# Norms by token halves, the first queries for 128 tokens first, and other homes for the gathered rows

## The chip, the core and the metric

The kernel runs on one core of one Trainium2 chip. The metric is its device time in microseconds (us). The core's engines are TensorE (PE; its weight loads are listed as PEld), VectorE (DVE), ScalarE (ACT), GpSimd (POOL) and SyncE (SP, which here only issues DMAs). A matrix product in full fp32 shows as two passes of PE; one in fp32r, on operands split into a high and a low part, as three products of one pass each.

## The reference

256 tokens of 1024 channels run through two layers (feed-forward, mixer, feed-forward), then one block of another kind, whose second half is an expert layer:

```python
for i in range(2):
    x = x + 0.5 * rmsnorm(swiglu_ffn(rmsnorm(x, pre1[i]), ...), post1[i])
    x = x + rmsnorm(mixer(rmsnorm(x, mix_pre[i])), mix_post[i])
    x = x + 0.5 * rmsnorm(swiglu_ffn(rmsnorm(x, pre2[i]), ...), post2[i])
h = rms_norm(x, norm1); merged = gated sum of mLSTM branch and RG-LRU branch
x = x + merged @ w_out
h2 = rms_norm(x, norm2)
q = h2 @ w_q                                # 8 heads, 2 x 128 each
scores = q . sub_keys                       # 128 keys for each half
idx, gate = best 16 of 16 x 16 sums         # per token and head
x = x + sum_k gate_k * gelu(u[idx_k] . h2) * v[idx_k]
out = rms_norm(x, final_norm)
```

With 8 heads of 16 experts each token needs 128 rows of `u` and 128 rows of `v`, each of 1024 fp32 numbers.

## The kernel before

Weights come in blocks of 1 MB (1024 x 256), each into one of `SLOTS` = 6 ring buffers `m.raw`; SP loads a block when the one six places earlier is used. `RING.first` gives a stage's first block. The residual lies by token, `m.x_tok[:, h, :]` with h the half of 128 tokens, and each half has two 512-channel parts d. All engines run programs written out in order (`tensor_program`, `scalar_program`, `vector_program`, `pool_program`, `sync_program`), joined by semaphores (`S.name.by` sets, `wait_ge(*S.name.at(...))` waits), so an instruction is late for all that is queued behind it on its engine.

**Seams.** At the end of a feed-forward or mixer the product is in PSUM banks 4 to 7, half 0 complete some us before half 1. `vector_post_norm` and `scalar_post_norm` (L646 to L681) take squares (ACT, L656), gain (DVE, L675), root (ACT, L659) and the residual add (DVE, L681), half after half. Then the residual is turned to channel-major by PE (`tensor_turn`, L752 to L767): for `mix` and `norm1` with a diagonal of the inverse norms (so the squares, `scalar_token_squares` L695, one root for both halves L706 and `vector_diagonals` L714 come first), for `pre1` and `pre2` plainly, where the norm follows as a row of factors after the first product block (`tensor_factor_row`, L721). `tensor_keep_going` (L743) lets PE multiply ones meanwhile: `before` products ahead of half 0's turn and `between` products ahead of half 1's. ACT makes the high part of the turned operand (`scalar_high`, L789), DVE the low part (`vector_low`, L797); the first product block (`tensor_split_block`, L451 to L453) waits for the low part of each pair of tiles. In layer stages `mix` the low parts of the weights are made by POOL (`pool_mix_rest`, L407), two blocks ahead and before the seam; in the FFNs by DVE (L443).

**The start.** SP issues x, two weight blocks and 22 small parameter loads. DVE makes mask constants (`vector_constants`, L531 to L545), PE turns the parameters when the last has landed (`tensor_params`, L613), runs 8 products of ones, and turns x.

**Output projection and queries.** `tensor_w_out` (L2273) multiplies half 0 by all four blocks of `w_out`, then half 1; DVE adds each half to the residual (L2329). Then the `norm2` seam for both halves, and `tensor_scores`: for each of 8 heads one block of `peer_w_q` times 256 tokens (L360), the turned `h` for the experts in quarters (L2375), and the scores (L2388), which ACT copies out (L2396). The weights of the queries come through the ring, each when a `w_out` or query block six places earlier is used.

**Experts.** `HEAD_TURNS` takes the 8 heads of half 0, then of half 1. `vector_choose` (L2470 to L2488, on DVE) makes one turn's 16 indices. `pool_experts` issues, for 32 groups of 8, the gathers of `u` rows of group i and then the `v` rows of group i-1 (L2539; one gather fetches one row for each of 128 tokens, 512 KB). DVE dots each `u` row with h (L2548); `v` rows are weighed and summed, four of each group by PE (L2641) and four by DVE (L2585). Row r goes to home r modulo the number of homes, and waits until the row before it there is done. There are 12 homes for `u` and 17 for `v` (`PeerMemory`): 16 in `m.proj`, 12 in ring slots that are free when a query block is used, one in `m.operand`. At group 0 DVE takes the first choice, then the second between its dots.

## Time and profile before

| | us |
|---|---|
| median of 3 runs (2656.16 to 2657.62) | 2656.24 |
| the profiled execution, its own time | 2657.05 |
| its span, first to last instruction | 2655.8 |

```profile
PE 2269.2 (85%) x13786; PEld 1932.1 (73%) x13786; DVE 1759.4 (66%) x3266; ACT 970.9 (37%) x1550; POOL 807.2 (30%) x671
...
PE   6999999999999999999999999999898544444445
...
DVE  5555894665556556894665555243429998989986
```

The first line gives busy time, share of the span and instruction count for each engine. The others cut the span into 40 slices of 66.4 us; a digit is the busy share of a slice in tenths. Waits are shown in brackets behind a timeline row: how long the engine had been idle and what released it. The granted clock of PE is given as a share of 2.4 GHz.

### The profile page before, as it was taken

The numbers are of one execution on the slowest core, as the hardware profiler recorded it, in microseconds if no ns is written. First come the engines' busy times: TensorE is split into PE (matmuls) and PEld (weight loads), VectorE is DVE, ScalarE is ACT, GpSimd is POOL, SyncE is SP. The second block draws the span as 40 slices with busy tenths as digits, with TensorE's granted clock in tenths as the row PEclk, the third lists the DMA queues.
The fourth block names the chain that finished last, engine by engine and source line by source line (L and its number), as shares of the span: only waits on it lengthen the run. The fifth ranks groups of instructions, "written<-read, shape, count | busy, mean of one in ns | idle before, by whom it ended". The sixth has DMA issues, their size and how long they took to land.

```text
span 2655.8 us, 34386 instructions
## 1 busy us (share of the span) xinstructions
PE 2269.2 (85%) x13786; PEld 1932.1 (73%) x13786; DVE 1759.4 (66%) x3266; ACT 970.9 (37%) x1550; POOL 807.2 (30%) x671
## 2 busy tenths in 40 slices
PE   6999999999999999999999999999898544444445
PEld 6998998998998998998998998888766211111111
DVE  5555894665556556894665555243429998989986
ACT  4345554454335435553454432342213111111111
POOL 1005772000000005771000000000007777777774
PEclk9999999999999999999999999999999677777767
DMA  6567994025554567993024554443249999999997
GB/s 212 183 179 129 188 167 131 33 74 177 183 183 160 188 171 129 187 174 117 33 94 155 184 190 144 141 139 106 74 150 399 419 419 419 419 418 418 419 419 314
DMA packets 316369, 560.29 MB, mean 211 GB/s; under 512 B 16296, under 2 KB 233394, under 8 KB 316210
## 3 DMA queue, kind: packets, MB, share of 16 engines
q1 hardware_dynamic: 242482, 289.63, 39.7%
q0 software_dynamic: 73728, 268.47, 24.9%
q8 instruction: 109, 1.79, 0.3%
q14 instruction: 50, 0.41, 0.1%
HBM read 557.00 MB, written 1.05 MB: 210 GB/s over the span
## 4 chain that ended last, share of the span: by engine, by line
PE 65%; DVE 13%; POOL 8%; DMA 7%; issue 3%; ACT 3%; SPq 0%; DVEq 0%; ACTq 0%; POOLq 0%
PE banks_to L853 11%; PE bank L451 7%; PE bank L452 7%; PE bank L453 7%; PE bank L360 6%; POOL proj L2539 5%; PE banks_and L360 4%; DMA proj<-in_peer_v,gdn_conv 4%; DMA weights<-in_peer_v,gdn_conv 3%; POOL weights L2539 3%; DVE banks_to L1054 3%; PE banks_and L451 3%; PE banks_and L452 3%; PE banks_and L453 3%; PE banks_to L1246 2%
## 5 line engine op out<-in xcount | busy, mean ns | idle before, releaser
L407 POOL TENSOR_TENSOR weights_low<-weights,weights_high 128x1024 fp32r<-128x1024 f32 x128 | 306.1, 2423 | 683.3 <-ACT weights_high L370 682.8
L453 PE MATMUL bank<-operand_hi,weights_low 128*128 128x256 f32 x1792 | 508.5, 284 | 0.0
L451 PE MATMUL bank<-operand_hi,weights_high 128*128 128x256 f32 x1776 | 505.2, 284 | 3.6 <-DVE operand_lo L797 3.3
L452 PE MATMUL bank<-operand_lo,weights_high 128*128 128x256 f32 x1776 | 503.6, 284 | 0.0
L370 ACT CAST weights_high<-weights 128x1024 fp32r<-128x1024 f32 x392 | 386.6, 1046 | 7.0 <-DMA weights<-in_ffn_w_in 6.7
L443 DVE TENSOR_TENSOR weights_low<-weights,weights_high 128x1024 fp32r<-128x1024 f32 x264 | 308.2, 1221 | 91.3 <-ACT weights_high L370 91.3
L451 PEld LDWEIGHTS bank<-operand_hi,weights_high 128*128 128x128 f32 x1776 | 339.1, 191 | 7.0 <-issue 4.7
L453 PEld LDWEIGHTS bank<-operand_hi,weights_low 128*128 128x128 f32 x1792 | 342.9, 191 | 0.0
L452 PEld LDWEIGHTS bank<-operand_lo,weights_high 128*128 128x128 f32 x1776 | 337.5, 190 | 1.3
L453 PE MATMUL banks_and<-operand_hi,weights_low 128*128 128x256 f32 x768 | 217.6, 283 | 0.0
L451 PE MATMUL banks_and<-operand_hi,weights_high 128*128 128x256 f32 x752 | 213.7, 284 | 3.6 <-DVE operand_lo L797 3.3
L452 PE MATMUL banks_and<-operand_lo,weights_high 128*128 128x256 f32 x752 | 212.7, 283 | 0.0
L2548 DVE CUSTOM_DVE_ANT_0 proj<-proj,banks_to 128x1024 f32<-128x1024 f32 x172 | 207.7, 1212 | 5.1 <-DMA proj<-in_peer_u,gdn_conv 4.9
L2539 POOL DMA_INDIRECT proj<-in_peer_u,gdn_conv x172 | 162.8, 947 | 90.0 <-issue 43.6
L2613 ACT ACTIVATE gdn_conv<-gdn_conv 128x8 f32<-128x8 f32 x32 | 6.7, 210 | 486.6 <-DVE gdn_conv L2548 486.6
L1054 DVE SCALAR_TENSOR_TENSOR banks_to<-proj,cnv_dw_cols,banks_to 128x254 f32<-128x254 f32 (+28 forms) x464 | 181.0, 472 | 0.0
L360 PE MATMUL bank<-operand,weights 128*128 128x256 f32 x736 | 161.8, 379 | 0.0
L2074 POOL TENSOR_TENSOR proj<-proj 128x512 f32<-128x512 f32 x4 | 5.6, 1420 | 493.9 <-ACT proj L2297 493.9
L360 PEld LDWEIGHTS bank<-operand,weights 128*128 128x128 f32 x736 | 139.4, 190 | 18.7
L451 PEld LDWEIGHTS banks_and<-operand_hi,weights_high 128*128 128x128 f32 x752 | 143.0, 190 | 5.1 <-issue 3.9
L453 PEld LDWEIGHTS banks_and<-operand_hi,weights_low 128*128 128x128 f32 x768 | 146.6, 191 | 0.0
L452 PEld LDWEIGHTS banks_and<-operand_lo,weights_high 128*128 128x128 f32 x752 | 142.5, 189 | 0.4
(524 smaller groups left out, 4402.6 us busy)
## 6 DMA issues: line engine op xcount, KB each, us to landing
weights<-in_ffn_w_in SPq DMA_DIRECT2D x88, 1024.0 KB, 5.1
weights<-in_mix_w_in SPq DMA_DIRECT2D x64, 1024.0 KB, 12.5
weights<-in_ffn_w_out SPq DMA_DIRECT2D x44, 1024.0 KB, 5.0
...
```

The costliest lines, as they stand in the source:

```text
L360: ins = t.matmul(out, raw[:, k, q * P:(q + 1) * P], x[:, k, :], start=(k == 0), stop=(k == KT - 1))
L370: S.high.by(X.scalar.copy(halves(high)[q], halves(m.raw[b % SLOTS])[q]), b, q)
L407: S.rest.by(X.gpsimd.tensor_tensor(halves(m.low[b % SLOTS])[q], halves(m.raw[b % SLOTS])[q], halves(mix_high(m, l, i))[q].bitcast(F32), AL ...
L443: S.low.by(X.vector.tensor_tensor(halves(m.low[b % SLOTS])[q], halves(m.raw[b % SLOTS])[q], halves(ffn_high(m, stage, i))[q].bitcast(F32), ...
L451: t.matmul(out, w_hi, x_hi, start=start, stop=False, skip_group_check=skip)
L452: t.matmul(out, w_hi, x_lo, start=False, stop=False, skip_group_check=skip)
L453: return t.matmul(out, w_lo, x_hi, start=False, stop=stop, skip_group_check=skip)
L853: ins = X.tensor.matmul(y_part(m, h, d), x(k)[:, at], w[:, k, d * 512:d * 512 + 512], start=start and k == 0 and n == 0, stop=last and k = ...
L1054: ins = v.scalar_tensor_tensor(out=acc(c)[:, s:NT], in0=glu(c)[:, 0:NT - s], scalar=weight(k, c), in1=acc(c)[:, s:NT], op0=ALU.mult, op1=A ...
L1246: ins = X.tensor.matmul(out[:, j, :], lhsT(j), rhs(j), start=True, stop=True)
L2539: landed[r % len(homes)].by(X.gpsimd.indirect_dma_start(out=home, out_offset=None, in_=table, in_offset=at), r)
L2548: S.dotted.by(X.vector.tensor_tensor_reduce(out=u, in0=u, in1=K.h_tok[:, n // HEADS, :], scale=1.0, scalar=0.0, op0=ALU.mult, op1=ALU.add, ...
```

## The change

It has these parts:

- **Token norms by halves.** Each half gets its own mean (on DVE), root (on ACT, with that mean as bias), reciprocal and diagonal. For `pre1` and `pre2` the roots and diagonals come ahead of the FFN's loop, no longer within it.
- **Order of the residual adds.** Half 1's gain goes between half 0's two adds.
- **Turn.** For `mix` and `norm1` no products of ones between the halves, 20 instead of 12 ahead, and tile pairs 0 and 1 of both halves before pairs 2 and 3. For `pre1` and `pre2` 10 ahead and 5 between instead of 8 and 8.
- **Entry block.** The first product block waits for each tile's high part, takes both products with it for both column halves, and takes the product with the low part of x last, over all tiles.
- **POOL** makes one mixer block's low part ahead of the seam, and the others after the last residual add of `post1`.
- **Start.** The second weight block is loaded behind the parameters; PE turns x and runs 12 products of ones before it turns the parameters; ACT squares x first; DVE makes its constants after the split of block 1. The parameters' columns go to banks 6, 7, 0, 1.
- **Output projection.** Half 0, then two of half 1's eight units, half 0's norm and turn and its first query (`tensor_half_turn`, `tensor_query_half`, `tensor_half_scores`, each for 128 tokens) between further units, then the rest. Three heads are done by halves. DVE takes choice 0 before it adds half 1 (`vector_output(X, m, S, 1)`).
- **Query weights 2 to 6** are loaded into `m.proj` when the last mLSTM output is made, ahead of `w_out`'s blocks 2 and 3; query 7 into the slot of `w_out`'s first block.
- **Homes.** `u` has 6 homes in `m.proj` and 4 in the slots of `w_out` blocks 1 and 2; `v` has 19, in the slots of `w_out` 3 and queries 0 and 1, the homes of query weights 2 to 6, the slot of `w_out` 0 with query 7's weights, and `m.operand`.

```diff
-GROUP, U_ROWS, V_ROWS = 8, 12, 17
+GROUP, U_ROWS, V_ROWS = 8, 10, 19
 DVE_ALONE, EARLY = 0, 2
...
+QUERY_HOMES = {2: 48, 3: 56, 4: 24, 5: 0, 6: 8}
+LAST_QUERY = 7
...
-        first = RING.first["peer_q", 2]
-        late = [(flat(m.raw[(first + j) % SLOTS][:, 4 * i:4 * i + 4, :]), first + j) for j in range(2, HEADS) for i in range(2)]
-        self.u = [(rows[:, s, :], None) for s in range(G)] + late[0:4]
-        self.v = [(rows[:, G + s, :], None) for s in range(G)] + late[4:12]
-        self.v += [(flat(m.operand[:, 0:4, :]), first + HEADS - 1)]
+        first, out = RING.first["peer_q", 2], RING.first["w_out", 2]
+        slot = lambda b: [(flat(m.raw[b % SLOTS][:, 4 * i:4 * i + 4, :]), b) for i in range(2)]
+        query = lambda n: [(rows[:, QUERY_HOMES[n] // 4 + i, :], first + n) for i in range(2)]
+        self.u = [(rows[:, s, :], None) for s in (4, 5, 8, 9, 10, 11)] + slot(out + 1) + slot(out + 2)
+        self.v = slot(out + 3) + slot(first) + slot(first + 1) + query(2) + query(3) + query(4) + query(5) + query(6)
+        self.v += [(home, first + LAST_QUERY) for home, _ in slot(out)] + [(flat(m.operand[:, 0:4, :]), first + LAST_QUERY)]
...
+def tensor_entry_block(X, m, S, b, high, low, n):
+
+    bank, x = b % BANKS, m.split_x
+    X.bank_free(bank)
+    out = lambda q: m.bank[bank][:, q * NT:(q + 1) * NT]
+    for q in range(2):
+        X.pe.wait_ge(*low.at(b, q))
+    for k in range(KT):
+        X.pe.wait_ge(*S.x_high.at(n, k))
+        for q in range(2):
+            hi, lo = halves(high)[q], halves(m.low[b % SLOTS])[q]
+            X.tensor.matmul(out(q), hi[:, k, :], x.hi[:, k, :], start=k == 0 and q == 0, stop=False, skip_group_check=True)
+            X.tensor.matmul(out(q), lo[:, k, :], x.hi[:, k, :], start=False, stop=False, skip_group_check=True)
+    for k in range(KT):
+        if k % 2 == 0:
+            X.pe.wait_ge(*S.x_low.at(n, k // 2))
+        for q in range(2):
+            ins = X.tensor.matmul(out(q), halves(high)[q][:, k, :], x.lo[:, k, :], start=False, stop=k == KT - 1, skip_group_check=True)
+    S.used.by(ins, b)
...
+def vector_gain_branch(X, m, S, n, ready, c, h):
+
+    v, w, gain, other = X.vector, X.dve, m.gain_row[GAIN_ROWS[n[0]]], m.sums[:, 2 * h + 1:2 * h + 2]
+    w.wait_ge(*ready[h])
+    for d in range(2):
+        _, at = part(h, d)
+        if d:
+            w.wait_ge(*S.squares_act.at(n, h, 1))
+            S.mean.by(v.tensor_scalar(other, other, mean_of(c), c * RMS_EPS, ALU.mult, ALU.add), n, h)
+        S.gained.by(v.tensor_tensor(m.spare_tok[:, h, at], y_part(m, h, d), gain[:, at], ALU.mult), n, h, d)
...
+    vector_gain_branch(X, m, S, n, ready, c, 0)
+    vector_add_branch(X, m, S, n, 0, 0)
+    vector_gain_branch(X, m, S, n, ready, c, 1)
+    vector_add_branch(X, m, S, n, 0, 1)
+    vector_add_branch(X, m, S, n, 1, 0)
+    vector_add_branch(X, m, S, n, 1, 1)
...
+def scalar_token_norm(X, m, S, n, ready, scratch):
+
+    scalar_token_squares(X, m, S, n, 0, ready, scratch)
+    scalar_token_squares(X, m, S, n, 1, ready, scratch)
+    scalar_token_root(X, m, S, n, 0)
+    scalar_token_root(X, m, S, n, 1)
...
-def tensor_boundary(X, m, S, n, first, ready, scaled, before, between):
+def tensor_boundary(X, m, S, n, first, ready, scaled, before):
 
     tensor_keep_going(X, m, before, first % BANKS)
-    tensor_turn(X, m, S, n, 0, first, ready, scaled)
-    tensor_keep_going(X, m, between, first % BANKS)
-    tensor_turn(X, m, S, n, 1, first, ready, scaled)
+    if scaled:
+        for pairs in ((0, 1), (2, 3)):
+            for h in range(2):
+                tensor_turn(X, m, S, n, first, ready, scaled, h, pairs)
+    else:
+        tensor_turn(X, m, S, n, first, ready, scaled, 0, range(4))
+        tensor_keep_going(X, m, before // 2, first % BANKS)
+        tensor_turn(X, m, S, n, first, ready, scaled, 1, range(4))
...
-            ins = X.scalar.activation(m.split_x.hi[:, k, :], m.bank[b][:, q * NT:(q + 1) * NT], ACT.Copy, scale=gain[:, k:k + 1])
-        S.x_high.by(ins, n, i)
+            S.x_high.by(X.scalar.activation(m.split_x.hi[:, k, :], m.bank[b][:, q * NT:(q + 1) * NT], ACT.Copy, scale=gain[:, k:k + 1]), n, k)
...
-            if j == 0:
-                scalar_token_root(X, m, S, pre_norm_of(stage))
...
-    sync_rows(X, m, S, first["w_out", 2], io["w_out_2"], 0)
+    sync_rows(X, m, S, first["w_out", 2], io["w_out_2"], 0, (0, 1))
+    X.sp.wait_ge(*S.mlstm_dve.at("y", 3))
+    for i, n in enumerate(QUERY_HOMES):
+        S.query_in[i].by(X.sync.dma_start(query_weights(m, n), columns(io["peer_w_q_2"], 0, n * 256)), n)
+    sync_rows(X, m, S, first["w_out", 2], io["w_out_2"], 0, (2, 3))
...
-    for i in range(HEADS):
+    for i in (0, 1):
         sync_load(X, m, S, first + i, columns(io["peer_w_q_2"], 0, i * 256))
+    X.sp.wait_ge(*S.used.at(RING.first["w_out", 2]))
+    S.query_in[-1].by(X.sync.dma_start(query_weights(m, LAST_QUERY), columns(io["peer_w_q_2"], 0, LAST_QUERY * 256)), LAST_QUERY)
     X.sp.wait_ge(*S.used.at(first + HEADS - 1))
...
+def tensor_output_and_scores(X, m, S, K):
+
+    units = [(i, k) for i in range(4) for k in range(2)]
+    tensor_w_out(X, m, S, 0, units)
+    tensor_w_out(X, m, S, 1, units[0:2])
+    tensor_half_turn(X, m, S, 0)
+    tensor_w_out(X, m, S, 1, units[2:3])
+    tensor_query_half(X, m, S, 0, 0)
+    tensor_w_out(X, m, S, 1, units[3:4])
+    tensor_half_scores(X, m, S, K, 0, 0)
+    tensor_w_out(X, m, S, 1, units[4:8])
+    for n in (0, 1):
+        tensor_turn_quarter(X, m, S, "h", m.operand, n, 4 + n)
+    tensor_query_half(X, m, S, 1, 0)
+    tensor_query_half(X, m, S, 2, 0)
+    tensor_half_scores(X, m, S, K, 1, 0)
+    tensor_half_turn(X, m, S, 1)
+    tensor_half_scores(X, m, S, K, 2, 0)
+    tensor_query_half(X, m, S, 0, 1)
+    tensor_query_half(X, m, S, 1, 1)
+    tensor_half_scores(X, m, S, K, 0, 1)
+    tensor_query_half(X, m, S, 2, 1)
+    tensor_half_scores(X, m, S, K, 1, 1)
+    for n in (2, 3):
+        tensor_turn_quarter(X, m, S, "h", m.operand, n, 4 + n)
+    tensor_query(X, m, S, HALVED)
+    tensor_half_scores(X, m, S, K, 2, 1)
+    for n in range(HALVED + 1, HEADS):
+        tensor_query(X, m, S, n)
+        tensor_head_scores(X, m, S, K, n - 1)
...
+def scalar_output_and_scores(X, m, S, K):
+    scratch, ready = m.early_sum[:, :].rearrange("p (t d) -> p t d", t=1).to_broadcast([P, 2, KT * P]), block_added_at(S)
+    scalar_token_squares(X, m, S, "norm2", 0, ready, scratch)
+    scalar_token_root(X, m, S, "norm2", 0)
+    scalar_half_operand(X, m, S, 0)
+    scalar_query_half(X, m, S, K, 0, 0)
+    scalar_half_scores(X, m, S, K, 0, 0)
+    scalar_query_half(X, m, S, K, 1, 0)
+    scalar_token_squares(X, m, S, "norm2", 1, ready, scratch)
+    scalar_token_root(X, m, S, "norm2", 1)
+    scalar_query_half(X, m, S, K, 2, 0)
+    scalar_half_scores(X, m, S, K, 1, 0)
+    scalar_half_operand(X, m, S, 1)
+    scalar_half_scores(X, m, S, K, 2, 0)
+    scalar_choose(X, m, S, K, 0)
+    scalar_query_half(X, m, S, K, 0, 1)
+    scalar_query_half(X, m, S, K, 1, 1)
+    scalar_half_scores(X, m, S, K, 0, 1)
+    scalar_query_half(X, m, S, K, 2, 1)
+    scalar_half_scores(X, m, S, K, 1, 1)
+    scalar_gelu(X, m, S, K, 0)
+    scalar_choose(X, m, S, K, 1)
+    scalar_query(X, m, S, K, HALVED)
+    scalar_half_scores(X, m, S, K, 2, 1)
+    scalar_gelu(X, m, S, K, 1)
+    for n in range(HALVED + 1, HEADS):
+        scalar_query(X, m, S, K, n)
+        scalar_head_scores(X, m, S, K, n - 1)
...
+def vector_output(X, m, S, h):
+    vector_add_output(X, m, S, h)
+    vector_token_mean(X, m, S, "norm2", h)
+    vector_diagonal(X, m, S, "norm2", h)
+    vector_half_operand(X, m, S, h)
...
-    X.dve.wait_ge(*S.score_pe.at("h", 3))
+    vector_output(X, m, S, 1)
+    X.dve.wait_ge(*S.score_pe.at("h", 1))
     choice = vector_choose(X, m, S, K, 1)
     for i in range(GROUPS):
         if i % 2 and i // 2 + 2 < CHOICES:
             choice = vector_choose(X, m, S, K, i // 2 + 2)
+        if i == HALF:
+            X.dve.wait_ge(*S.score_pe.at("h", 3))
...
-    sync_ffn(X, m, S, ("ffn1", 0), 0, io["ffn1_w_in"], io["ffn1_w_out"], range(AHEAD))
+    sync_ffn(X, m, S, ("ffn1", 0), 0, io["ffn1_w_in"], io["ffn1_w_out"], range(1))
     sync_layer_params(X, m, S, io, 0)
+    sync_ffn(X, m, S, ("ffn1", 0), 0, io["ffn1_w_in"], io["ffn1_w_out"], range(1, AHEAD))
...
-    tensor_params(X, m, S, 0)
     for l in range(LAYERS):
-        tensor_to_split(X, m, S, ("pre1", l), ("ffn1", l), x_ready_at(S, l), False, 8, 8 if l else 0)
-        tensor_ffn(X, m, S, ("ffn1", l), split_at(S, ("pre1", l)))
+        tensor_to_split(X, m, S, ("pre1", l), ("ffn1", l), x_ready_at(S, l), False, 10 if l else 0)
+        if not l:
+            tensor_keep_going(X, m, 12, 1)
+            tensor_params(X, m, S, 0)
+        tensor_ffn(X, m, S, ("ffn1", l))
         y_taken(X, S, ("post1", l))
-        tensor_to_split(X, m, S, ("mix", l), ("glu", l), added_at(S, ("post1", l)), True, 12, 8)
+        tensor_to_split(X, m, S, ("mix", l), ("glu", l), added_at(S, ("post1", l)), True, 20)
...
 def vector_program(X, m, S, K):
-    vector_constants(X, m, S)
     vector_split(X, m, S, ("ffn1", 0), 0)
     vector_params(X, m, S, 0)
     first = RING.first
...
         X.dve.wait_ge(*columns_at(S, l))
         vector_low(X, m, S, ("pre1", l), first["ffn1", l], g(0))
+        vector_token_norm(X, m, S, ("pre1", l))
         if not l:
             vector_split(X, m, S, ("ffn1", l), 1)
+            vector_constants(X, m, S)
         vector_ffn(X, m, S, ("ffn1", l))
...
-        for i in range(AHEAD):
-            pool_mix_rest(X, m, S, l, i)
-        for i in range(AHEAD, MIX_BLOCKS):
+        pool_mix_rest(X, m, S, l, 0)
+        X.pool.wait_ge(*S.added_dve.at(("post1", l), 1, 1))
+        for i in range(1, MIX_BLOCKS):
```

`tensor_half_turn` turns one half with its diagonal into banks 2 and 3 (16 passes), `scalar_half_operand` and `vector_half_operand` scale four tiles of 128 columns each, `tensor_query_half` is one query block for 128 tokens (32 passes), `tensor_half_scores` the 4 score passes of a half, and the `scalar_...` functions of the same names copy them out.

## Rows read from the trace of the kernel before

**Rows 1.** The page: DMA rate in 40 slices, and the chain's shares.
```profile
GB/s 212 183 179 129 188 167 131 33 74 177 183 183 160 188 171 129 187 174 117 33 94 155 184 190 144 141 139 106 74 150 399 419 419 419 419 418 418 419 419 314
PE 65%; DVE 13%; POOL 8%; DMA 7%; issue 3%; ACT 3%; SPq 0%; DVEq 0%; ACTq 0%; POOLq 0%
```

**Rows 2.** Windows: length, busy us (count) by engine, PE clock, DMA share, GB/s.
```profile
1996.00:2004.00 8.00, 8.00 (x43) 7.15 (x42) 7.79 (x27) 2.45 (x3) 6.17 (x7) 1.00 0.99 376
2100.00:2200.00 100.00, 44.72 (x80) 17.42 (x79) 91.43 (x209) 13.08 (x33) 75.58 (x81) 0.74 1.03 419
```

**Rows 3.** Timeline, projection to first gather: start, us, instruction, [idle before <-releaser].
```profile
1932.80 27.63 PE L2273 MATMUL banks_to<-weights,branch 128*128 128x512 f32 x64
1963.28 0.48 DVE L714 TENSOR_SCALAR stat<-ident,norm_factors 128x128 f32<-128x128 f32 x2
1968.19 7.07 PE L360 MATMUL banks_and<-operand,weights 128*128 128x256 f32 x32
1977.82 0.29 DVE L2470 COPY gdn_conv<-gdn_conv 128x256 f32<-128x256 f32 x1 [8.47 <-ACT gdn_conv L2396]
1988.21 1.17 POOL L2539 DMA_INDIRECT proj<-in_peer_u,gdn_conv  x1 [37.87 <-DVE gdn_conv L2488]
1992.94 1.22 DVE L2548 CUSTOM_DVE_ANT_0 proj<-proj,banks_to 128x1024 f32<-128x1024 f32 x1 [4.88 <-DMA proj<-in_peer_u,gdn_conv]
```

**Rows 4.** Timeline of dots (DVE L2548) and gathers (POOL L2539) in two places.
```profile
2005.91 1.21 DVE L2548 CUSTOM_DVE_ANT_0 proj<-proj,banks_to 128x1024 f32<-128x1024 f32 x1
2007.11 1.17 POOL L2539 DMA_INDIRECT proj<-in_peer_u,gdn_conv  x1 [0.30 <-issue]
...
2385.26 1.20 DVE L2548 CUSTOM_DVE_ANT_0 proj<-proj,banks_to 128x1024 f32<-128x1024 f32 x1
2389.67 0.94 POOL L2539 DMA_INDIRECT weights<-in_peer_u,gdn_conv  x1 [0.30 <-issue]
```

**Rows 5.** Timeline, end of layer 0's first FFN to the mixer's first product.
```profile
209.56 7.11 POOL L407 TENSOR_TENSOR weights_low<-weights,weights_high 128x1024 fp32r<-128x1024 f32 x3
215.20 2.68 DVE L681 SCALAR_TENSOR_TENSOR residual<-spare,norm_factors,residual 128x512 f32<-128x512 f32 x2
215.66 2.84 PE L743 MATMUL bank<-ones 128*128 128x128 f32 x24
223.14 0.73 PE L763 MATMUL banks_and<-stat,residual 128*128 128x128 f32 x4 [4.64 <-DVE stat L714]
230.99 0.36 PE L451 MATMUL bank<-operand_hi,weights_high 128*128 128x256 f32 x1 [0.59 <-DVE operand_lo L797]
```

**Rows 6.** Timeline, norm1, before the second part of the network.
```profile
1607.48 1.41 DVE L681 SCALAR_TENSOR_TENSOR residual<-spare,norm_factors,residual 128x512 f32<-128x512 f32 x2
1619.21 1.08 PE L1819 MATMUL banks_to<-operand,gdn_conv 128*100 128x256 f32 x4
```

**Rows 7.** Timeline, pre2 of layer 0, into its second FFN.
```profile
618.56 0.84 ACT L789 ACTIVATE operand_hi<-banks_and,param_cols 128x256 fp32r<-128x256 f32 x2 [2.20 <-PE banks_and L765]
620.46 0.36 PE L451 MATMUL banks_and<-operand_hi,weights_high 128*128 128x256 f32 x1 [1.28 <-DVE operand_lo L797]
628.34 0.71 PE L721 MATMUL banks_and<-stat,ones 128*128 128x128 f32 x4 [1.79 <-DVE stat L714]
```

**Rows 8.** Windows, columns as in rows 2.
```profile
224.00:227.50 3.50, 3.50 (x20) 3.50 (x20) 0.00 (x0) 0.00 (x0) 0.00 (x0) 0.55 0.96 87
629.00:634.00 5.00, 5.00 (x32) 5.00 (x31) 3.25 (x4) 2.57 (x4) 0.00 (x0) 0.66 0.37 152
```

**Rows 9.** Timeline, the start.
```profile
6.72 0.29 DVE L536 TENSOR_TENSOR gdn_conv<-gdn_conv 128x128 int32<-128x128 int32 x1 [6.72 <-POOL gdn_conv L528]
15.93 0.97 PE L613 MATMUL banks_to<-ident,param_rows 97*128 97x97 f32 x4 [15.93 <-DMA head_params<-in_gdn_dt_bias]
22.87 0.36 PE L451 MATMUL bank<-operand_hi,weights_high 128*128 128x256 f32 x1 [1.42 <-DVE operand_lo L797]
46.08 0.63 PE L853 MATMUL banks_to<-weights_high,ffn_gated_hi 128*128 128x512 f32 x2
```

321 lines of the change are left out of this document (182 added, 139 removed).

## Prediction

> **What bounds the kernel now.** I read the slices of the page first. Up to slice 29 of 40 the DMAs move 33 to 212 GB/s; from slice 31 they stand at 399 to 419, till the last [rows 1]. The chain of waits says what the part before is bound by: 65% of the span is on TensorE (PE), then 13% VectorE (DVE), 8% POOL, 7% DMA [rows 1]. So there are two regimes: a PE-bound part up to the output projection, and the expert stage, bound by 512 gathers of 512 KB. Then the windows: in full stream 419 GB/s is one gather each 1.25 us, DVE is busy 91% of it, and POOL (an issue every 1.24 us) is never the last to be ready [rows 2, 4]. Hence an instruction is worth its time in two places only: at the seams where PE stands still, and before the first gather at 1988.21, since from there 512 x 1.25 us follow almost whatever is done. The timelines of the seams are the third view [rows 3, 5 to 9].
>
> **The sum** is made against the profiled execution: span 2655.8, time 2657.05, which is 0.8 over the median 2656.24.
>
> **Output projection to the first gather.** Before: 64 projection passes from 1932.80 at 0.43 us, so until 1960.4, the second half's residual add, norm, turn, a whole query block from 1968.19, scores, a copy, and only then the first choice, from 1977.82, which ends in the gather at 1988.21 [rows 3]. After: the first token half is full at 1932.8 + 32 x 0.43 = 1946.6, as before. Its own norm chain (add, two squares, root, reciprocal, diagonal) took 3.2 us for the second half (1960.4 to the first diagonal's end at 1963.6 [rows 3]); it lies beside 8 passes of the second half, which end at 1950.0. Behind these on PE: 16 turn passes of 128 columns at 0.12 (24 fill passes of that size took 2.84 [rows 5]) = 1.9; 4 projection passes = 1.7; a query half, 32 passes at 0.12 = 3.9; 4 projection passes = 1.7; 4 score passes = 0.5. The scaling by ACT and DVE hides behind the 1.7s. With copy and semaphores 0.9 the choice starts at about 1960.6: 17.2 us sooner, and so does the first gather. The added norm instructions, each half's own mean, root, reciprocal, are counted in the 3.2.
>
> That isn't the gain yet. Only after the choice does DVE add the second half (0.7 x 2); PE has by then 16 projection passes (6.9), 8 quarter turns (1.0), two query halves (7.8), scores (0.5) and the second turn (1.9) to do from 1959.8, so until 1978; then DVE scales four tiles (1.2). First dot about 1979.3, against 1992.94 [rows 3]: 13.6 sooner. And u has 10 homes instead of 12: the 16th u row must wait for the sixth dot. Before, that dot ended at 2007.12 and the row was issued at 2007.11 [rows 4], so with ten homes it would just have passed; now the gathers are 3.6 us further ahead of the dots, so POOL stands about 3.5 us at rows 12 to 16, and 13.5 is what is left at the issue. Some of the rest comes back: before, the first gathers shared the DMAs with query weights (376 GB/s in 1996 to 2004 against 419 [rows 2]); now those lie in their homes before. **15 us, between 12 (the second half comes 1.5 later than I reckon) and 17.2.** In steady stream the closest place has 3.1 us between a dot's end (2385.26 + 1.2, with its read 2386.6) and the row that takes ten homes later (2389.67) [rows 4], so two homes fewer cost nothing there. The five query blocks that SP now issues before the last two output blocks are 5 MB; at the 419 GB/s that the engines reach [rows 2] that is 13 us, in a stretch with 74 GB/s of other traffic (slice 29 [rows 1]); the last output block is issued one product block (some 7 us) before 1932.8 and wanted 10 us after it. Cost: nothing. SP's wait for the mLSTM outputs ends before the load ahead of it is due. The last query block comes when the first output block is used, about 1950, 70 us before use.
>
> The Trainium skill (TensorE: Matmul & The Clock Gate, Back-to-back issue gap) gives some 81 ns for a sustained matmul of 128 columns where the rows here have 120. By it the query half would be an estimated 2.6 us and the first gather 2 us earlier still. The trace has the duration for this data type, and the sum uses that.
>
> **Two mix entries.** PE's last projection pass is issued before 215.66, then 24 fill passes, then it stands 4.64 us until the first diagonal (223.14), turns half 0, runs 16 fill passes, turns half 1, and the first product starts at 230.99, on the low part [rows 5]: 15.3 us. New: POOL waits with its second block until the residual is added. Beside POOL's subtractions (209.56, 7.1 us for three) two adds took 2.68 where norm1's took 1.41 with POOL at rest [rows 5, 6]; so 1.3 off, plus 0.3 from the new order of adds: first diagonal at 221.5. No fill between, and pairs in an order that lets ACT begin after 12 of 32 passes: the turn ends at 221.5 + 32 x 0.12 = 225.4, and the product starts there, as it now asks only for the high part of its tile (ACT 0.42 per tile [rows 7], PE four passes of 0.12) and takes the low parts last. **5.5 us each.** If PE runs at 1.2 GHz in the turn, 32 passes take 3.5 us longer: then 3 or less each, if the turn before had the full rate; it had not, as below. POOL's second block is due 5.8 us after the first product and takes 4.9 from 219.7: hidden with 6 us to spare. Taken 5.3, from 3 to 5.6.
>
> Of the clock the rows say: PE had stood still for 4.64 us before the first turn pass, and the clock granted in 224 to 227.5 is 0.55, 1.2 GHz for most of it [rows 5, 8]. With 40 fill passes of 0.12 it would stand 1.1. The Trainium skill (TensorE: Matmul & The Clock Gate, Part 1) says that an idle array falls to half rate and activity releases it; by it the new seam holds 2.4 GHz, and by the row behind a 1.8 us stop (0.66 of the clock in 629 to 634 [rows 7, 8]) it may not. The range holds both.
>
> **norm1**: same seam without POOL: the adds end at 1608.9, the order saves 0.3, squares' rest, root and diagonal take 1.8, so the turn runs from 1610.4 to 1614.4 with no fill in it, and products follow, which came at 1619.21 [rows 6]. **4.6**, from 2.5 to 5.
>
> **Three pre-norm entries** (pre2 twice, pre1 of layer 1). High parts begin at 618.56, the first product at 620.46, the factor row at 628.34, for which PE stood 1.79 [rows 7]. New: residual 0.3 earlier; product on the high part at 618.8: 1.7 sooner, and block 0 ends about 624.7. The roots now come straight behind the squares and ahead of the next block's split: diagonals at 625.2 instead of 628.3. **3.1 each**, from 2 to 4.8 (where a half-rate stretch behind the stop goes too). The split that is moved back is due a block (5.8 us) later and ends 3 us ahead of that.
>
> **The start.** Params are issued by SP behind one block instead of two; the last lands at 15.93 and first products come at 22.87, after 16 fill passes and the turn [rows 9]. Now the turn is done while the params load: params, 1.0 on PE, 1.4 on DVE, then ACT 0.4: product at 17 to 18, or at 15.5 if the 1 MB that goes behind them frees the queue. But DVE's constants (23 instructions of some 0.26 with what lies between them, from 6.72 [rows 9], so 5.9) now lie between block 1's split and everything of the FFN: block 2's low part comes at 33, the first gated product's low part at about 42.3 where PE waits for it; before, PE began on it at 46.1 [rows 9]. Gain **4.5**, from 1.5 to 7.
>
> **Sum**: 15 + 2 x 5.3 + 4.6 + 3 x 3.1 + 4.5 = 44.0. 2657.05 - 44.0 = 2613.0; 0.8 less for the median: **2612**. With all low ends 12 + 6 + 2.5 + 6 + 1.5 = 28, 2628; with all high ends 17.2 + 11.2 + 5 + 14.4 + 7 = 54.8, 2601.5.
>
> **Rivals.**
> (1) The earlier gathers find DVE too slow: it is 91% busy in the stream [rows 2], has the second half's add and norm in front of it, and the ten homes tie POOL to it. The stream then gains only what DVE's work order allows, 4 instead of 15: 2623, with other low ends up to 2634. Against it: DVE itself starts 13.6 sooner and has 9% to catch up in.
> (2) The seams give half: the clock falls in the turns, and the start is eaten by the constants: 15 + 6 + 2.5 + 6 + 0 = 29.5: 2627.
> (3) Slower: u reuse. If a u row finds its home in use in every group, the stream loses that each time and the DMAs run dry. The margin of 3.1 us [rows 4] is the point from which it decides; 2 us past it in each of some 30 groups is 60 us, against 44 gained: 2672. For it: 12 rows of home were 15 us of stream, ten are 12.4. Against it: most rows have more than the closest one, and v gets the two homes.
> (4) It doesn't do what it says: the first half's scores wait for the whole projection after all (a bank or the copy order). Then the first gather gains 8, not 17: inside (1).
> (5) Better: PE keeps 2.4 GHz everywhere and the stream keeps the full 17.2: under 2600.
>
> **Chances.** Forecast 0.74 (its own range 2601 to 2628), (1) with (4) 0.12, (2) alone 0.07, (5) 0.04, (3) 0.03. Range 2598 to 2631: it leaves out (3), half of (1) and part of (5). 0.2% (5.3 us) is about what a measurement of this kernel can tell from no change; only (3) reaches there: faster 0.95, same 0.02, slower 0.03.
>
> **What would show it.** First gather at about 1988.2 - 29 (earlier seams) - 17 = 1942, first dot 9 us behind it; a POOL wait on a DVE dot of 3 to 4 us around the 12th to 16th gather; 419 GB/s from then on; PE's stop before the mix turns near 1 us and ACT's first high part 1.6 us behind the diagonal; factor row 6.5 us behind the first product. Wrong would be: POOL waits on dots in every group, PE waits on a query's operand, w_out products waiting for a DMA, or a start in which PE waits 5 us and more for gated products.

## The result, and the profile after

The changed kernel takes 2610.5 us (median of four runs, 2609.0 to 2611.3), the kernel before 2656.9 beside it: ratio 0.982, 95% interval 0.981 to 0.984. That is 46.4 us; forecast were 44 (2612, range 2598 to 2631). The profiled execution has a span of 2609.7 and a time of 2610.97, so the sum can be checked term by term against the spans: 2655.8 - 2609.7 = 46.1.

The page after, DMA rate in 40 slices and the shares of the chain:

```profile
GB/s 224 192 170 136 190 174 124 33 71 185 186 186 170 186 172 138 186 177 119 33 74 173 192 179 166 140 133 109 109 201 393 419 419 419 419 419 419 420 419 314
PE 66%; DVE 13%; POOL 9%; DMA 5%; issue 4%; ACT 3%; DVEq 0%; POOLq 0%; ACTq 0%
```

Beside [rows 1] nothing has changed its kind: a part bound by PE, then the stream at 419 GB/s.

**The part bound by PE.** Each seam begins with PE's fill passes, so their starts mark the stages. First five of them before (the first, 215.66, and the start of the output projection, 1932.80, stand in [rows 5, 3]); columns are start, us, instruction:

```profile
613.70 1.95 PE L743 MATMUL banks_and<-ones 128*128 128x128 f32 x16
811.91 1.95 PE L743 MATMUL banks_and<-ones 128*128 128x128 f32 x16
1008.17 2.84 PE L743 MATMUL banks_and<-ones 128*128 128x128 f32 x24
1406.48 1.95 PE L743 MATMUL bank<-ones 128*128 128x128 f32 x16
1604.59 2.84 PE L743 MATMUL bank<-ones 128*128 128x128 f32 x24
```

and all of them after, with the projection's first row:

```profile
210.44 4.63 PE L807 MATMUL bank<-ones 128*128 128x128 f32 x40
604.60 2.39 PE L807 MATMUL banks_and<-ones 128*128 128x128 f32 x20
799.25 2.39 PE L807 MATMUL banks_and<-ones 128*128 128x128 f32 x20
991.90 4.63 PE L807 MATMUL banks_and<-ones 128*128 128x128 f32 x40
1386.23 2.39 PE L807 MATMUL bank<-ones 128*128 128x128 f32 x20
1580.47 4.63 PE L807 MATMUL bank<-ones 128*128 128x128 f32 x40
1902.51 17.33 PE L2344 MATMUL banks_to<-weights,branch 128*128 128x512 f32 x40
```

The lead over the kernel before grows 5.2, 9.1, 12.7, 16.3, 20.3, 24.1, 30.3. The differences are the terms:

| term | forecast | found |
|---|---|---|
| the start | 4.5 | 5.2 |
| the two mixer entries | 5.3 + 5.3 | 3.9 + 4.0 |
| the three pre-norm entries | 3 x 3.1 | 3.6 + 3.6 + 3.9 |
| norm1 (and what stands behind it to the projection) | 4.6 | 6.2 |
| sum before the projection | 29.0 | 30.3 |
| projection, first gather, homes | 15 | 15.8 |

**The output projection and the stream**, where [rows 3, 4] stood:

```profile
1919.68 1.95 PE L2471 MATMUL banks_and<-stat,residual 128*128 128x128 f32 x16
1923.18 3.73 PE L2499 MATMUL bank<-operand,weights 128*128 128x128 f32 x32
1928.47 0.61 PE L2534 MATMUL banks_and<-spare,ffn_silu 128*128 128x128 f32 x4
1929.59 0.29 DVE L2677 COPY gdn_conv<-gdn_conv 128x256 f32<-128x256 f32 x1 [6.72 <-ACT gdn_conv L2553]
1939.97 1.17 POOL L2746 DMA_INDIRECT proj<-in_peer_u,gdn_conv  x1 [19.91 <-DVE gdn_conv L2695]
1947.28 1.21 DVE L2755 CUSTOM_DVE_ANT_0 proj<-proj,banks_to 128x1024 f32<-128x1024 f32 x1
1956.71 0.94 POOL L2746 DMA_INDIRECT proj<-in_peer_u,gdn_conv  x1 [0.67 <-DVE gdn_conv L2755]
1959.23 0.94 POOL L2746 DMA_INDIRECT proj<-in_peer_u,gdn_conv  x1 [1.58 <-DVE gdn_conv L2755]
1961.68 0.94 POOL L2746 DMA_INDIRECT proj<-in_peer_u,gdn_conv  x1 [1.50 <-DVE gdn_conv L2755]
2600.01 1.29 DVE L2792 SCALAR_TENSOR_TENSOR banks_and<-proj,gdn_conv,banks_and 128x1024 f32<-128x1024 f32 x1 [1.17 <-DMA proj<-in_peer_v,gdn_conv]
```

The first gather comes 37.5 us behind the projection's start instead of 55.4: 17.9 sooner. POOL then stands at the 14th, 15th and 16th gather for a dot that frees its home. Over the usual 1.24 us from one issue to the next [rows 2] that is 0.4 + 1.3 + 1.2 = 2.8 us. From the first gather to the last add of DVE it takes 660.0 us; before it took 657.9, the last add being this row of before:

```profile
2646.15 1.29 DVE L2585 SCALAR_TENSOR_TENSOR banks_and<-proj,gdn_conv,banks_and 128x1024 f32<-128x1024 f32 x1 [1.16 <-DMA proj<-in_peer_v,gdn_conv]
```

So 17.9 - 2.1 = 15.8 of it reach the end.

### The profile page after: what moved, and what is told of

Same layout as the page of the kernel before. It is cut to its first block, busy times and chain, and to the rows that moved or that the text cites. A ratio compares the mean times of both kernels' runs of the same rounds, so it can differ in the third digit from the quotient of the medians.

```text
span 2609.7 us, 34589 instructions
## 1 busy us (share of the span) xinstructions
PE 2258.9 (87%) x13860; PEld 1925.0 (74%) x13860; DVE 1763.8 (68%) x3286; ACT 974.1 (37%) x1568; POOL 806.9 (31%) x671
## 4 chain that ended last, share of the span: by engine, by line
PE 66%; DVE 13%; POOL 9%; DMA 5%; issue 4%; ACT 3%; DVEq 0%; POOLq 0%; ACTq 0%
PE banks_to L923 11%; PE bank L457 7%; PE bank L458 6%; PE bank L459 6%; PE bank L366 6%; POOL proj L2746 5%; POOL weights L2746 4%; PE banks_and L366 4%; DVE banks_to L1125 3%; DMA proj<-in_peer_v,gdn_conv 3%; PE banks_and L457 3%; PE banks_and L458 3%; PE banks_and L459 2%; PE banks_to L1317 2%; DMA weights<-in_peer_v,gdn_conv 2%
## 5 line engine op out<-in xcount | busy, mean ns | idle before, releaser
L459 PE MATMUL bank<-operand_hi,weights_low 128*128 128x256 f32 x1744 | 493.5, 283 | 0.0
L457 PE MATMUL bank<-operand_hi,weights_high 128*128 128x256 f32 x1728 | 489.8, 283 | 0.3 <-DVE gdn_conv L1210 0.2
L458 PE MATMUL bank<-operand_lo,weights_high 128*128 128x256 f32 x1728 | 488.9, 283 | 0.0
L459 PE MATMUL banks_and<-operand_hi,weights_low 128*128 128x256 f32 x720 | 203.5, 283 | 0.0
L457 PE MATMUL banks_and<-operand_hi,weights_high 128*128 128x256 f32 x704 | 198.9, 283 | 2.2 <-DVE weights_low L449 2.0
L2755 DVE CUSTOM_DVE_ANT_0 proj<-proj,banks_to 128x1024 f32<-128x1024 f32 x156 | 188.4, 1213 | 1.1 <-DMA proj<-in_peer_u,gdn_conv 0.9
L2746 POOL DMA_INDIRECT proj<-in_peer_u,gdn_conv x156 | 146.9, 942 | 70.0 <-issue 41.2
L2848 PE MATMUL banks_to<-proj,branch 128*128 128x512 f32 x128 | 76.8, 751 | 89.2 <-DMA proj<-in_peer_v,gdn_conv 89.2
L2848 PE MATMUL bank<-proj,branch 128*128 128x512 f32 x136 | 79.4, 742 | 74.0 <-DMA proj<-in_peer_v,gdn_conv 74.0
L2746 POOL DMA_INDIRECT proj<-in_peer_v,gdn_conv x133 | 126.8, 953 | 40.6 <-issue 39.7
```

What stands on the lines that cost most here:

```text
L457: t.matmul(out, w_hi, x_hi, start=start, stop=False, skip_group_check=skip)
L458: t.matmul(out, w_hi, x_lo, start=False, stop=False, skip_group_check=skip)
L459: return t.matmul(out, w_lo, x_hi, start=False, stop=stop, skip_group_check=skip)
L2746: landed[r % len(homes)].by(X.gpsimd.indirect_dma_start(out=home, out_offset=None, in_=table, in_offset=at), r)
L2755: S.dotted.by(X.vector.tensor_tensor_reduce(out=u, in0=u, in1=K.h_tok[:, n // HEADS, :], scale=1.0, scalar=0.0, op0=ALU.mult, op1=ALU.add, ...
L2848: ins = t.matmul(pe_sum(m, half)[c][:, :], K.diag[p][:, s, :], K.v[r % len(K.v)][0][:, c * 512:c * 512 + 512], start=(i == first and s == ...
```

## Experiments

All are the changed kernel with one edit, or with two where it says so. "The control" is the changed kernel measured again, in one group with "both together", the second run with 12 and 17 homes and the one with 8 and 21. The four runs of the last two headings are a group of their own without a control, and the kernel before took 2656.7 in it against 2655.5 beside the control; measured by the kernel before, each of their distances to the control is 1.2 us smaller than the plain difference that is given. Seams are read in each run's trace, since from one execution to the next a stretch at half clock somewhere can be worth more than an edit.

### The control

> The kernel after, unchanged: the control for the runs of this group. Where the kernel before takes 2657 as in the first comparison, this one takes 2610.5 (ratio 0.9824); where it takes 2824, as in the group of runs before this one, this one lies at about 2697 (0.955), since three kernels with the same homes were at 0.953 to 0.955 there.

Measured: 2610.4 us, 0.983 of the kernel before (0.982 to 0.984). In its trace the mixer entry takes 11.41 us from fills to first product, as in the first profile, and the last add comes 659.7 behind the first gather.

### POOL's wait in the mixer entries

The mixer entries gained 3.9 where I had 5.3. The timeline of the changed kernel around the first one:

```profile
212.88 1.41 DVE L720 SCALAR_TENSOR_TENSOR residual<-spare,norm_factors,residual 128x512 f32<-128x512 f32 x2
214.37 4.65 POOL L413 TENSOR_TENSOR weights_low<-weights,weights_high 128x1024 fp32r<-128x1024 f32 x2 [7.62 <-DVE residual L720]
215.46 1.33 DVE L773 TENSOR_SCALAR stat<-ident,norm_factors 128x128 f32<-128x128 f32 x1
216.90 2.19 DVE L773 TENSOR_SCALAR stat<-ident,norm_factors 128x128 f32<-128x128 f32 x1
219.15 0.71 PE L829 MATMUL banks_and<-stat,residual 128*128 128x128 f32 x4 [1.14 <-DVE stat L773]
221.85 0.36 PE L488 MATMUL bank<-operand_hi,weights_high 128*128 128x256 f32 x1
```

POOL is held back until the last residual add, and those adds are fast (1.41 for two). Then it starts, right in front of the two diagonals, which take 1.33 and 2.19; in norm1, with POOL at rest, they take 0.29 each. The first diagonal ends at 216.79, as POOL's second subtraction begins, and the second diagonal at 219.09, as that subtraction ends:

```profile
216.67 2.34 POOL L413 TENSOR_TENSOR weights_low<-weights,weights_high 128x1024 fp32r<-128x1024 f32 x1
```

The 128x1 reciprocals between them keep their 0.16 and 0.15 us. The contention has moved one step down the same chain. Two edits tell it apart.

```diff
-        X.pool.wait_ge(*S.added_dve.at(("post1", l), 1, 1))
+        X.pool.wait_ge(*S.diagonal.at(("mix", l), 1))
```

> The kernel after, with POOL's wait in the mixer entries moved from the last residual add to the second diagonal. In the kernel after POOL starts its second block at 214.37 in layer 0, and the two diagonals beside it take 1.33 and 2.19 us instead of the 0.29 and 0.29 of norm1, which has no POOL; the first product comes 11.41 us after the fills begin against 9.05 in norm1. Theory: that contention is why the mix seams gained 3.9 instead of 5.3 us. Diagonals then take 0.3 each, and each of two entries gains 2.3: 2605.9. Rival: POOL's second and third blocks come 1.9 us later and PE waits for them (the second is due at 227.8 and would be ready at about 221 to 223): the gain is given back, 2610.5. Third: the diagonals are slow for another reason; no change in their duration, 2610.5.

```diff
-        pool_mix_rest(X, m, S, l, 0)
-        X.pool.wait_ge(*S.added_dve.at(("post1", l), 1, 1))
-        for i in range(1, MIX_BLOCKS):
+        for i in range(MIX_BLOCKS):
```

> The kernel after, with POOL's wait in the mixer entries taken out, so that POOL makes blocks 0 and 1 ahead as before. The prediction valued this wait at 1.3 us a seam: by it the kernel is 2.6 slower, 2613.1, with residual adds at 2.7 for two instead of 1.4. Rival: the wait ends too early and its POOL work slows the diagonals by 2.9 us; without it POOL is done before them, so the adds lose 1.3 or less and the diagonals win 2.3 each seam: 2 faster, 2608.5. If both the adds and the diagonals are free of POOL: 2606.

These two, the next one and the first run on the homes ran where the gathers moved 375 GB/s in full stream and the kernel before took 2824.0 us; so their times are compared with that, and their seams with those of the other runs, since PE's passes have the same durations there. Measured: 2692.9 (0.953, 0.952 to 0.955) and 2696.6 (0.955, 0.954 to 0.957). These times don't separate the two, nor either from a control, which that group lacked. The traces do. From fills to first product: 8.96 us with the wait on the diagonal (210.00 to 218.96), 10.11 with no wait (208.18 to 218.29), 11.41 in the changed kernel. In the run without the wait:

```profile
202.08 7.11 POOL L413 TENSOR_TENSOR weights_low<-weights,weights_high 128x1024 fp32r<-128x1024 f32 x3
207.72 2.02 DVE L720 SCALAR_TENSOR_TENSOR residual<-spare,norm_factors,residual 128x512 f32<-128x512 f32 x1
211.77 1.41 DVE L720 SCALAR_TENSOR_TENSOR residual<-spare,norm_factors,residual 128x512 f32<-128x512 f32 x2
214.35 0.29 DVE L773 TENSOR_SCALAR stat<-ident,norm_factors 128x128 f32<-128x128 f32 x1
```

one add is slowed to 2.02 and the diagonals are not. So in this entry the wait as it stands costs 1.3 us, where the forecast had it saving 1.3. In layer 1's entry the same run took 11.76 us, though its diagonals were as fast (0.28 and 0.29), since its turn ran partly at half clock. Its first turn passes, and a window of the turn (length, PE busy us, granted clock, DMA share, GB/s):

```profile
991.59 0.71 PE L829 MATMUL banks_and<-stat,residual 128*128 128x128 f32 x4 [1.91 <-DVE stat L773]
993.00:996.00 3.00, 3.00 (x16) 0.50 0.99 84
```

So over both entries, 10.11 + 11.76 against 2 x 11.4, the wait cost 1.0 us; taking it out is not a sure 1.3 each. The wait on the diagonal gave 8.96 in both entries: put one step later it is worth 2.4 more in each. The Trainium skill (SBUF — State Buffer, SBUF: two separate sides) says that DVE and POOL share a pair of ports, an exclusive lock: a POOL instruction, or a DVE instruction that runs in a 2-port mode or has two inputs in SBUF, holds it to its end and blocks the other. The rows agree, in that a diagonal of 0.29 beside POOL subtractions of 2.3 each takes up to 2.19 and ends right behind one of them.

### DVE's constants in the start

PE waits for DVE twice in the changed kernel's start:

```profile
15.99 0.36 PE L488 MATMUL bank<-operand_hi,weights_high 128*128 128x256 f32 x1 [1.78 <-ACT operand_hi L860]
30.31 0.39 PE L457 MATMUL banks_and<-operand_hi,weights_high 128*128 128x256 f32 x1 [1.95 <-DVE weights_low L449]
39.20 0.95 PE L923 MATMUL banks_to<-weights_high,ffn_gated_hi 128*128 128x512 f32 x2 [2.91 <-DVE ffn_gated_lo L1012]
```

```diff
+        yield                                    # vector_constants, behind each level
...
-            vector_constants(X, m, S)            # vector_program, behind the split of block 1
...
+    constants = vector_constants(X, m, S) if stage == ("ffn1", 0) else iter(())
...
             w.wait_ge(*S.silu_scaled.at(stage, j))
+            if j >= 2:
+                next(constants, None)            # one mask level, three instructions
             w.wait_ge(*S.used.at(first + i))
```

> The kernel after, with DVE's 23 instructions for masks no longer between the second weight block's split and the first FFN, but one level (three instructions, 0.75 us) in each of the FFN's later groups, where DVE waits up to 3.8 us for PE's products. Theory: the two waits of PE on DVE in the start (1.95 us at 30.31, 2.91 us at 39.20) and the half clock behind the second (about 1.0) come from these 5.7 us alone: 4.9 to 5.9 faster, 2605.1. Rival: ACT's split, not DVE's, is what PE would wait for next: 2 to 3 faster, 2608. Slower only if the spread instructions delay a gated product in a later group: 2611 or more.

Measured: 2694.0 (0.954, 0.953 to 0.956) on the slower gathers, between the two runs above, so the times of that group show no gain. In its trace both waits are gone, and the first output block begins at

```profile
33.84 0.63 PE L924 MATMUL banks_to<-weights_high,ffn_gated_hi 128*128 128x512 f32 x2
```

with its fills of the mixer entry at 203.4, against 207.9 to 210.4 in the changed kernel and the other runs so far: 4.5 to 7.0. The constants cost what the theory says, and ACT is not next in line.

### Both together

> The kernel after with both edits that the traces bear out: POOL's wait on the second diagonal (in the trace of that run the first product of a mixer came 8.96 us behind the fills instead of 11.41) and DVE's mask constants spread over the first FFN's later groups (the first output block of the FFN at 33.84 instead of 39.20, the fills of the mixer entry at 203.4 instead of 208 to 210.4). Sum: 2 x 2.45 + 4.5 to 7.0 = 9.4 to 11.9 below the control, 2600 where the control is 2610.5. Rival: part of it is given back where the stretches at half clock fall (3.4 us each came and went between the runs in the middle of the first mixer): 5 to 8 below.

Measured: **2601.65** us (2600.6 to 2602.5), 0.980 of before (0.978 to 0.981), 8.8 below the control. Fills and turn of its first mixer entry:

```profile
204.15 4.63 PE L808 MATMUL bank<-ones 128*128 128x128 f32 x40
209.52 0.71 PE L830 MATMUL banks_and<-stat,residual 128*128 128x128 f32 x4 [0.75 <-DVE stat L774]
```

The start gives 6.2 against the control (210.30), the two entries 2.4 each, together 11.1; 1.4 went in the first mixer, between its first product and the next fills (384.2 against 382.8), and 0.3 behind norm1, so that the projection begins 9.4 earlier. It beats both kernels. This is the rival's course in a small size, and the granted clock shows where the 1.4 lies. Two windows of this run, then the same two places in the control (length, PE busy us and passes, granted clock, DMA share, GB/s):

```profile
347.00:355.00 8.00, 8.00 (x44) 0.57 0.68 210
412.00:420.00 8.00, 8.00 (x29) 0.79 0.40 132
356.00:364.00 8.00, 8.00 (x56) 0.79 0.64 202
421.00:429.00 8.00, 8.00 (x22) 0.57 0.30 107
```

The stretch at half clock is long in the first place and short in the second, in the control the other way round. Wherever it was so, this stage took 384.2 us (here and in the run on the turn below), and 382.7 to 382.9 with the control's pattern. Why the pattern changes the runs don't show.

### How the homes are dealt out

```diff
-GROUP, U_ROWS, V_ROWS = 8, 10, 19
+GROUP, U_ROWS, V_ROWS = 8, 12, 17
-... + slot(out + 1) + slot(out + 2)                  # u
-        self.v = slot(out + 3) + slot(first) + ...
+... + slot(out + 1) + slot(out + 2) + slot(out + 3)  # u
+        self.v = slot(first) + ...
```

> The kernel after (median 2610.5), with 12 u homes and 17 v homes: the two halves of the fourth output block's buffer go from v to u. Theory of the forecast: the only price of ten u homes is POOL's standing at the 14th, 15th and 16th gather (0.37 + 1.28 + 1.20 = 2.8 us in the kernel after). It goes, the last add comes 657.9 us behind the first gather as before instead of 660.0, and the time falls by 2.1 to 2.8 us, to 2608.0. Rival: DVE is the bound of the first groups, so the dots are late whatever the homes, the wait turns up a few rows later and the time stays at 2610.5 (within 0.7). Second rival: 17 v homes are now too few, because v rows wait longer for their use when u runs further ahead: slower, 2613 or more, with POOL waits on v's users.

> The kernel after with 12 u homes and 17 v homes, again, now beside the unchanged kernel after. If full stream stands at 419 GB/s: the forecast's theory says that POOL's 2.8 us of standing at the 14th to 16th gather go and the time is 2.1 to 2.8 below the control; the rival (the dots are late anyway) says no difference; the rival of scarce v homes says 3 us and more above it. If the gathers come slower, at 270 to 390 GB/s as in the group before: 70 us above the control, since 17 v homes hold POOL back whenever landings are late.

Measured: first 2766.1 (0.980, 0.978 to 0.981) on the slower gathers, 72 above the three kernels of its group with ten and 19; then, beside the control, 2617.4 (0.986, 0.984 to 0.987), **7.0 above** it. The forecast's theory got the wait on dots right (it goes) and the sign wrong. In the second run's trace POOL stands further on:

```profile
1989.02 0.99 POOL L2746 DMA_INDIRECT proj<-in_peer_v,gdn_conv  x1 [4.22 <-PE bank L2511]
1996.82 0.94 POOL L2746 DMA_INDIRECT weights<-in_peer_v,gdn_conv  x1 [5.57 <-PE bank L2511]
```

These are v rows 12 and 14, and with 17 homes theirs are the buffers of query blocks 6 and 7, which PE reads until about 1988.7 and 1996.5 (PE rows of 7.07 from 1981.67 and 1989.47):

```profile
1981.67 7.07 PE L2511 MATMUL bank<-operand,proj 128*128 128x256 f32 x32
1989.47 7.07 PE L2511 MATMUL bank<-operand,weights 128*128 128x256 f32 x32
```

Two stops, 4.3 and 5.3 over the pitch, less the 2.8 that went: 6.8 us, and the last add comes 666.5 behind the first gather instead of 659.7. With 19 homes these buffers are due two rows later, and the rows fall behind PE's release (in the control query block 6 is read until 1990.2, and its row is issued at 1991.81). So without the pair of homes in v 7 of the 15.8 us that reach the end would be lost; the forecast priced it at nothing.

The 72 us on the slower gathers are another matter. There POOL waited on dots all through the stream: with ten homes for u and 19 for v at 23 to 35 gathers, 32 to 48 us in all over the usual pitch, with 12 and 17 at 44 gathers, 115 us. The second run's expectation, that 17 homes for v hold POOL back, isn't what these waits name, and more homes for u didn't shorten them; how 17 homes for v make the dots late I haven't shown.

```diff
-GROUP, U_ROWS, V_ROWS = 8, 10, 19
+GROUP, U_ROWS, V_ROWS = 8, 8, 21      # slot(out + 2) goes to v too
```

> The kernel after with 8 u homes and 21 v homes. The margin of the prediction: the closest place of the steady stream had 3.1 us with ten homes, so 0.6 with eight (two rows of 1.24 less): by it no stall in the steady stream, only a longer wait at the start, rows 9 to 16, of 2.8 + 2.5 = 5.3 us: 2.5 above the control, 2613. Rival 3 of the prediction (reuse of u homes stalls every group, and each stall is lost): 2 us in each of 30 groups, 60 above the control. In between, if a few groups pass the point: 5 to 20 above.

Measured: 2616.1 (0.985, 0.984 to 0.987), 5.7 above the control. POOL stands at six gathers, the 11th to 16th, 7.3 us in all, 4.5 more than the control, and the last add comes 664.2 behind the first gather, 4.5 more. No stall on a dot follows in the rest of the 512. So at 419 GB/s two homes less than ten still cause none in steady stream, and rival 3 is refuted for that rate; at 375 GB/s, as just said, POOL did wait on dots with ten. What I had wrong is the start, where dots are 2.5 us apart (a choice lies between them), so each missing home adds a row that stands 1.2 to 1.5.

### The order of the first choice and the second half

```diff
+    vector_add_output(X, m, S, 1)
+    vector_token_mean(X, m, S, "norm2", 1)
+    vector_diagonal(X, m, S, "norm2", 1)
     for _ in vector_choose(X, m, S, K, 0):
         pass
-    vector_output(X, m, S, 1)
+    vector_half_operand(X, m, S, 1)
```

> The kernel after, with DVE adding and normalising the second token half ahead of the first choice instead of behind it. Theory: what makes the first gather early is that the choice waits for nothing of the second half. DVE then waits for the last projection pass (1936.0 against the choice's start at 1929.59 now), adds, makes the diagonal, and chooses from about 1938.9: first gather at 1949.3 instead of 1939.97, 9.3 later; POOL's standing of 2.8 at the 14th to 16th gather goes, as the dots start at once: 6.5 to 9.3 slower, 2617 to 2619.7. Rival: the stream is bound by the dots, which now start 4 sooner: no slower than 2612.

Measured: 2620.7 (0.986, 0.985 to 0.988), 10.3 above the control. The first gather:

```profile
1956.97 1.17 POOL L2746 DMA_INDIRECT proj<-in_peer_u,gdn_conv  x1 [33.17 <-DVE gdn_conv L2695]
```

is 50.7 us behind the projection's start (1906.24) instead of 37.5: 13.3 later, 4 more than I expected, since DVE stood 4.1 us for ACT's squares, which wait in ACT's queue behind a query copy. POOL's standing went, and 2.3 came back in the stream. So the place of the first choice ahead of the second half is worth most of the 17.9, some 4 of the 13.3 through ACT's queue, which this edit left as it was.

### The turn, the entry block, the params

```diff
-        for pairs in ((0, 1), (2, 3)):
-            for h in range(2):
-                tensor_turn(X, m, S, n, first, ready, scaled, h, pairs)
+        tensor_turn(X, m, S, n, first, ready, scaled, 0, range(4))
+        tensor_keep_going(X, m, 8, first % BANKS)
+        tensor_turn(X, m, S, n, first, ready, scaled, 1, range(4))
```

> The kernel after, with the scaled turn (two mixer entries and norm1) by token halves again, all four pairs of half 0, 8 fill passes, all four pairs of half 1, instead of two pairs of both halves and then the other two. Theory by rows: in the mixer entries the second diagonal comes 2.3 us behind the first, so 1.9 of turn and 1.0 of fill nearly fit before it, and the product comes at 221.7 against 221.85: no change; in norm1, where the diagonals come together, the fill costs 1.0. Sum 1.0: 2611.4, within 1 of the control. The forecast's view (the order of pairs lets ACT begin after 12 of 32 passes, and no fill lies in the turn): 1.5 a seam, 4.5 slower, 2614.9.

Measured: 2612.3 (ratio 0.983, 0.982 to 0.984, the control's): the times can't tell it from the control. In the trace the mixer entries take 11.8 instead of 11.4, norm1 11.1 instead of 9.05: 2.8 in all, between the two theories. The order of pairs was worth little in the mixer, where the second diagonal was late anyway, and 2 us in norm1.

```diff
-        X.pe.wait_ge(*S.x_high.at(n, k))      # tensor_entry_block, tile by tile
+    for k in range(0, KT, 2):                 # ahead of the first product
+        X.pe.wait_ge(*S.x_low.at(n, k // 2))
```

> The kernel after (control 2610.4), with the first block of every stage waiting for all low parts of its tile before its first product, as before, its passes in the new order. Theory of the forecast: what the high-first order gives is the way from the first high part to the last low part. In the kernel after the first product of the mixer comes at 221.85 and the last low part ends at 224.22: 2.4 later in each of two entries; 1.7 in each of three pre-norm entries (what the forecast valued); 3.5 at the start (15.99 against 19.55). Sum 4.8 + 5.1 + 3.5 = 13.4: 2623.8. Rival: PE would have stood anyway behind the entry (for the factor row, or for DVE's constants in the start, which are the bound there), so only the mixer's part and half of the others count: 7 slower, 2617.5.

Measured: 2629.2 (0.990, 0.989 to 0.992), 18.8 above the control, not 13.4. The edit is harsher than the kernel before: there the products waited for the low parts pair by pair (PE stood 1.28 in [rows 7]), here for all. PE stands 3.6 us in the pre-norm entries, not 1.7, and 5.5 in the start, and what follows is at half clock. Row and window (length, PE busy us, granted clock, DMA share, GB/s) of this run:

```profile
613.82 0.55 PE L489 MATMUL banks_and<-operand_hi,weights_high 128*128 128x256 f32 x1 [3.63 <-DVE operand_lo L868]
614.00:617.00 3.00, 3.00 (x15) 0.50 0.00 0
```

and the control in the same entry, with no stop:

```profile
610.00:613.00 3.00, 3.00 (x27) 1.00 0.00 0
```

The 5.5 us in the start cost nothing in the end: the fills of the first mixer entry come at 208.1, within the 207.9 to 210.4 of the other runs and 2.2 earlier than in the control, so there the expectation's rival held (PE would have stood for DVE's constants anyway). From there to the projection, fills to fills, the stages lose 2.6, 3.4, 4.9, 5.6 and 3.7. So going on with the high parts is worth its wait and the clock behind it. As a price of the part alone this run is an upper bound.

```diff
-    sync_ffn(..., range(1))
+    sync_ffn(..., range(AHEAD))
     sync_layer_params(X, m, S, io, 0)
-    sync_ffn(..., range(1, AHEAD))
```

> The kernel after, with SP issuing the first layer's params behind two weight blocks instead of one, as before. Theory: the params land where they did before (15.93 against 13.7 now), the first product comes 2.3 later (18.2), and everything of the start shifts with it: 2.3 slower, 2612.7. Rival: DVE's constants bound the start (PE waits for DVE twice, 4.9 us in all), but they too come behind the params' copies on DVE, so nothing is absorbed; if ACT and DVE did get further ahead in that time, 0 to 1 slower: 2611.

Measured: 2614.0 (0.984, 0.983 to 0.986), 3.6 above the control. The first product comes at 18.17 instead of 15.84, the mixer's fills 2.2 later, norm1's 2.1 later; the rest lies behind norm1 in that execution. Nothing was absorbed.

## Why the prediction held, and where it was off

**The stream term** (15, found 15.8). First gather 17.2 sooner: 17.9. First dot 9 us behind it: 7.3. POOL 3 to 4 us at the 12th to 16th gather: 2.8, at the 14th to 16th. The 419 GB/s came as said. The arithmetic in passes of 0.43 and 0.12 held because nothing but PE stood in that chain. What failed is a sentence: "v gets the two homes" stood only as a point against rival 3, with no price for v without them. The runs put 7 us on it, with POOL waiting for query buffers, a wait that my list of what would be wrong did not hold.

**Mixer entries** (5.3 each, found 3.9 and 4.0). Mis-sized: "POOL wait saves 1.3". I took the diagonals at norm1's 0.29 while I had POOL start its 4.9 us of work at 219.7, in front of them. PE's stop before the turn was 1.79 and not 1, and a second of 1.14 came in the turn. ACT's first high part came 3.1 us behind the first diagonal, not 1.6. The clock, which I feared for, stayed at 1.00. With the contention gone an entry takes 8.96 instead of 15.3, a gain of 6.4: the rest of the term was sized 1 us too low, and the two errors partly hid each other.

**norm1** (4.6, found 6.2). Fills to first product took 9.05; by my times it was 10.0. The turn began 5.4 us behind the fills where I had 5.8, and the product followed 3.7 behind its first pass where I had 4.0. That and 0.6 further on, where the trace shows no single cause.

**Pre-norm entries** (3.1, found 3.6 to 3.9): up to the factor row no stop of PE is left, the 1.79 there included (PE goes straight on to the row at 615.64; I had left 0.5), and the row comes 5.8 us behind the first product where I had 6.5. By the factor row each entry is 3.6 us ahead. The half clock behind the old stop, which I had only in the upper bound, went too (1.00 in 604 to 620), but it paid little: from the factor row to the first gated product pre2 of layer 0 takes 13.9 us in both kernels, since PE now stands there for DVE's copies of the next parameters:

```profile
629.58 0.73 PE L923 MATMUL banks_to<-weights_high,ffn_gated_hi 128*128 128x512 f32 x2 [1.41 <-DVE cnv_dw_cols L658]
```

In layer 1 this new stop is 0.90, and 0.4 of the half clock comes back.

**The start** (4.5, found 5.2): product at 15.99, the early end of my two; PE then waits 4.9 us for DVE, behind the constants. The 5.2 is one execution's: in the other runs with this start and the product at 15.1 to 15.8 the fills came at 207.9 to 210.3, a gain of 5.3 to 7.7, so the closeness to 4.5 is partly luck. The two kernels with the constants spread gave 11.5 and 12.2 here.

**Rivals.** (1) and (4) are out: the first gather kept its gain to within 2.1. (2) is out, seams gave 30.3 of 29. (3) is refuted down to eight homes where the gathers move 419 GB/s. (5) was missed by 10 us. The sum was right within 2.1 us, partly since the errors cancel (-2.7 in the mixer entries; +1.7, +1.6, +0.7 and +0.8 in the others).
